# A hybrid attention and mLSTM layer in fp32: the first token tile's norm and its gains' way onto the partitions

## The reference

```
def rms_norm(x, g):
    xf = x.astype(jnp.float32)
    y = xf * lax.rsqrt(jnp.mean(xf * xf, axis=-1, keepdims=True) + EPS)
    return (y * g.astype(jnp.float32)).astype(x.dtype)
...
    xn = rms_norm(h, norm_mix[l])
    proj = xn @ w_in[l]
```

## Time and profile before

| | us |
|---|---|
| median of 3 runs | 950.24 |
| lowest, highest | 948.61, 951.85 |
| profiled execution, its time | 950.14 |
| profiled execution, its span | 948.4 |
| TensorE busy | 936.2 (99% of the span) |
| VectorE busy | 544.2 (57%) |
| ScalarE busy | 415.6 (44%) |
| GpSimd busy | 14.7 (2%) |

### The profile page before, as it was taken

How to read it: one execution, slowest core, us unless ns; L and a number is a source line. 1 busy time by engine, 2 the same in 40 slices (tenths; PEclk the granted TensorE clock), 3 DMA queues, 4 the chain that set the end, 5 groups by cost and what they waited for, 6 DMA issues and landing times.

```text
span 948.4 us, 11911 instructions
## 1 busy us (share of the span) xinstructions
PE 936.2 (99%) x4667; PEld 764.4 (81%) x4667; DVE 544.2 (57%) x942; ACT 415.6 (44%) x694; POOL 14.7 (2%) x39
## 2 busy tenths in 40 slices
PE   8999999999999999999999999999999999999997
PEld 6878777777777878889988778998888888888886
DVE  5532676343546763778333534568847866885543
ACT  5431566344423333344434533366446445634523
POOL 4000000000000000000000000000000000000000
PEclk9999999999999999999999999999999999999999
DMA  8411221122111272342521242120531261062202
GB/s 292 134 46 44 89 90 45 45 89 89 45 45 45 89 258 77 130 135 92 198 89 39 97 175 83 51 89 1 178 134 45 89 222 45 1 207 104 89 1 88
DMA packets 44815, 92.62 MB, mean 98 GB/s; under 512 B 1772, under 2 KB 1864, under 8 KB 44760
## 3 DMA queue, kind: packets, MB, share of 16 engines
q1 hardware_dynamic: 43192, 86.54, 27.1%
q0 software_dynamic: 1568, 5.32, 1.7%
HBM read 89.76 MB, written 2.10 MB: 97 GB/s over the span
## 4 chain that ended last, share of the span: by engine, by line
PE 94%; DVE 3%; ACT 1%; DMA 1%; issue 0%; SPq 0%; ACTq 0%; DVEq 0%
PE bank L1442 70%; PE bank L1473 12%; PE bank L1647 1%; PE bank L1598 1%; PE bank L1541 1%; PE bank L1568 1%; PE bank L1553 1%; PE bank L1486 1%; DVE w_lo L1046 1%; PE bank L1585 1%; PE bank L1625 1%; PE bank L1612 1%; DMA stage<-in_w_in 1%; PE bank L1586 0%; PE bank L1543 0%
## 5 line engine op out<-in xcount | busy, mean ns | idle before, releaser
L1046 DVE TENSOR_TENSOR w_lo<-stage,w_hi 128x1024 fp32r<-128x1024 f32 x174 | 205.0, 1220 | 87.5 <-ACT w_hi L763 87.1
L1442 PE MATMUL bank<-act_hi,w_hi 128*128 128x512 f32 (+1 forms) x640 | 248.3, 388 | 0.1
L1442 PE MATMUL bank<-act_hi,w_lo 128*128 128x512 f32 (+1 forms) x640 | 243.4, 380 | 0.0
L1442 PE MATMUL bank<-act_lo,w_hi 128*128 128x512 f32 (+1 forms) x640 | 243.1, 380 | 0.0
L763 ACT ACTIVATE w_hi<-stage 128x1024 fp32r<-128x1024 f32 x174 | 174.3, 1051 | 96.0 <-PE bank L1442 36.0
L1442 PEld LDWEIGHTS bank<-act_hi,w_lo 128*128 128x128 f32 x640 | 120.7, 189 | 23.3
L1442 PEld LDWEIGHTS bank<-act_hi,w_hi 128*128 128x128 f32 x640 | 121.1, 189 | 22.1 <-DVE w_lo L1046 0.6
L1442 PEld LDWEIGHTS bank<-act_lo,w_hi 128*128 128x128 f32 x640 | 121.0, 189 | 21.4
L1442 PE MATMUL bank<-w_hi,act_hi 128*128 128x512 f32 (+1 forms) x264 | 103.5, 392 | 3.2 <-DVE act_lo L1264 3.2
L1442 PE MATMUL bank<-w_hi,act_lo 128*128 128x512 f32 (+1 forms) x264 | 101.6, 385 | 0.0
L1442 PE MATMUL bank<-w_lo,act_hi 128*128 128x512 f32 (+1 forms) x264 | 101.6, 385 | 0.0
(11 more groups left out here) (276 smaller groups left out, 1261.4 us busy)
## 6 DMA issues: line engine op xcount, KB each, us to landing
stage<-in_w_in SPq DMA_DIRECT2D x20, 1024.0 KB, 5.0
stage<-in_w_mlp_in SPq DMA_DIRECT2D x16, 1024.0 KB, 5.2
stage<-in_w_mlp_out SPq DMA_DIRECT2D x16, 1024.0 KB, 5.5
stage<-in_w_xkv SPq DMA_DIRECT2D x8, 1024.0 KB, 4.9
stage<-in_w_mix_out SPq DMA_DIRECT2D x4, 1024.0 KB, 5.0
stage<-in_w_xq SPq DMA_DIRECT2D x4, 1024.0 KB, 5.1
stage<-in_w_xo SPq DMA_DIRECT2D x4, 1024.0 KB, 4.9
x_tok<-in_x SPq DMA_DIRECT2D x4, 512.0 KB, 9.7
```

What stands on the lines that cost most here:

```text
L1046: dve.tensor_tensor(w_lo[:, r:r + 2, :], stage_pair(pair), w_hi[:, r:r + 2, :].bitcast(F32), ALU.subtract).then_inc(s_low, 1)
L1442: ins = pe.matmul(dst, still[q], moving[q], start=(k == 0 and q == 0), stop=(k == nk - 1 and q == 2))
```

## The change

Tile 0 alone takes another way. VectorE multiplies x by the gains as soon as both are there, without the root (`scale_first`). The root then goes into a 128x128 matrix `eye`, the identity with each row times its root, and TensorE multiplies each 128x128 block of the scaled tile by `eye`, which turns it and applies the root in one fp32 product. The gains of all four tiles are no longer spread by the DMA: ScalarE's queue loads one row of 4 KB into one partition of `row_a`, and TensorE multiplies it by a row of ones into banks 6 and 7, from which VectorE reads them. The 15 first products become 6 ahead of the spread, 4 behind it and 2 behind the turned tile. GpSimd's six small transfers wait until the last x tile has landed.

```
-WARM_UP = 15
+WARM_UP = (6, 4, 2)
...
             load_x(0)
-            sp.dma_start(row_a[:], norm_mix.partition_broadcast(P)).then_inc(s_row_x, 16)
...
+            pool.wait_ge(s_xt[NT - 1], 16)
             small(w16[:, :, 0:8], w_in[:, C_FF:C_FF + 8].rearrange("(k p) n -> p k n", p=P))
...
+            act.dma_start(row_a[0:1, :], norm_mix.rearrange("(o n) -> o n", o=1)).then_inc(s_gains, 16)
             act.wait_ge(s_eps, 1)
...
+            def scale_first(n):
+                dve.wait_ge(s_xt[n], 16)
+                for h in range(2):
+                    c = slice(HALF_W * h, HALF_W * (h + 1))
+                    dve.wait_ge(s_row_x, h + 1)
+                    dve.tensor_tensor(scaled[:, n, c], x_tok[:, n, c], bank[6 + h][:], ALU.mult).then_inc(s_scaled, 1)
+
             def norm_root(n):
                 st = stat[:, n % 2, :]
+                if n == 0:
+                    scale_first(n)
                 dve.wait_ge(s_squares, n + 1)
...
             def norm_scale(n):
                 st = stat[:, n % 2, :]
+                if n == 0:
+                    dve.wait_ge(s_const, N_IDENT)
+                    dve.tensor_scalar(eye[:], ident[:], st[:, 2:3], None, ALU.mult).then_inc(s_eye, 1)
+                    return
+                if n < NT:
+                    for h in range(2):
+                        c = slice(HALF_W * h, HALF_W * (h + 1))
+                        dve.scalar_tensor_tensor(scaled[:, n % 2, c], x_tok[:, n, c], st[:, 2:3], bank[6 + h][:],
+                                                 ALU.mult, ALU.mult).then_inc(s_scaled, 1)
+                    return
...
                 if n == 0:
-                    pe.wait_ge(s_const, N_IDENT)
+                    pe.wait_ge(s_eye, 1)
+                    for b in range(2):
+                        for q in range(4):
+                            k = 4 * b + q
+                            ins = pe.matmul(bank[2 + b][:, P * q:P * q + P], scaled[:, 0, P * k:P * k + P], eye[:],
+                                            start=True, stop=True)
+                        ins.then_inc(s_nturn, 1)
+                    for _ in range(WARM_UP[2]):
+                        pe.matmul(bank[5][:, 0:P], ones[:], ones[:], start=True, stop=True)
+                    return
...
             pe.wait_ge(s_const, 1)
-            for _ in range(WARM_UP):
+            for _ in range(WARM_UP[0]):
                 pe.matmul(bank[7][:, 0:P], ones[:], ones[:], start=True, stop=True)
+            pe.wait_ge(s_gains, 16)
+            for h in range(2):
+                pe.matmul(bank[6 + h][:], ones[0:1, :], row_a[0:1, HALF_W * h:HALF_W * (h + 1)], start=True, stop=True)\
+                  .then_inc(s_row_x, 1)
+            for _ in range(WARM_UP[1]):
+                pe.matmul(bank[5][:, 0:P], ones[:], ones[:], start=True, stop=True)
```

More of the change, by code:

```diff
@@ L423, in trunk @@
         second_sum = sb("second_sum", [P, 1])
+        eye = sb("eye", [P, P])
         first_bias = sb("first_bias", [P, NT])
@@ L505, in trunk @@
         s_residual = sem("s_residual")
+        s_gains, s_eye = sem("s_gains"), sem("s_eye")
         s_row_x, s_row_a, s_row_b = sem("s_row_x"), sem("s_row_a"), sem("s_row_b")
@@ L852, in norm @@
                 c = slice(0 if n < NT + 2 else HALF_W if n < 4 * NT + 1 else HALF_W + EDGE, DM)
-                act.activation(junk[:, n % 2, c], norm_source(n)[:, c], ACT.Square, accum_out=stat[:, n % 2, 0:1])\
+                act.activation(junk[:, 1 if n == 0 else n % 2, c], norm_source(n)[:, c], ACT.Square, accum_out=stat[:, n % 2, 0:1])\
                     .then_inc(s_squares, 1)
```

## The result

Over 22 executions each the median is 951.93 us (950.5 to 955.68) with the change and 949.49 (948.55 to 951.85) before. The ratio is 1.0023, with a 95% interval of 1.0015 to 1.003: slower by 0.23%, within the 0.3% that was called "same". The profiled execution with the change took 954.1 us against 950.14, so it lost 4.0 us where the medians lie 2.4 apart. Both figures need an explanation.

The account below looks back on a forecast made before the run. TensorE holds 94% of the chain of waits, but a ScalarE and VectorE series ends the first 24 products. The second `act_hi` comes 1.64 us later, other terms count nothing: 950.14 + 1.64 = 951.8 us, range 948.7 to 953.6.

Parts of the forecast that it names:

- first part: First 20 us: a chain of ScalarE and VectorE, not TensorE's rate, ends the first two halves' 24 products.
- step 5: ScalarE's second `act_hi` starts at 10.98 instead of 9.34; the first 24 products end 1.64 us later.
- Steps 1 and 2: TensorE's start: six `ones` products until 3.60, then the gains' spread, 3.4 us until 7.00, with 0.21 of drain.
- Step 3: VectorE: multiply stands before the root; second multiply from 7.23, root 0.83, `eye` 0.28, ready at 8.98.
- Step 4: TensorE's turned tile: 16 records at full clock, 1.94 us from 9.02 to 10.96; 3.6 below full clock.
- rival B: TensorE's clock stays low until after the turned tile, 3.6 not 1.94 us: +3.3, 953.4; chance 0.15.
- The case of the forecast: The spread sits in front of VectorE's root, turned tile at full clock: 951.8; chance 0.62.
- Step 6: Removed 512 KB transfer: first weights land at about 6.5, but nothing is gained, since VectorE is busy until 8.98.
- Step 7: Full clock behind the turned tile saves seven products 1.4 us, lost waiting for the fourth `w_lo`: counted as nothing.
- Steps 2 and 8: Spread 3.4 us; delayed small transfers cost nothing; gains from PSUM -0.1 to +0.1 per half, hidden behind TensorE.

Follow-up runs that it names:

- e1: Changed kernel with TensorE's spread and late small transfers kept, but tile 0 scaled and transposed as before: 950.41 us against 950.16 for the kernel before, ratio 1.0.
- e2: Changed kernel without the spread: gains by the 512 KB transfer again, tile 0 still turned by products with `eye`; 951.78 us, ratio 1.0023 to the kernel before.
- e5: Changed kernel with tile 0's root and `eye` ahead of the multiply and no `ones` between spread and turned tile: 952.48 us, ratio 1.0019 to the kernel before.
- e9: Changed kernel with the spread taken over all 128 rows, `row_a` zeroed first: 952.9 us, ratio 1.003 to the kernel before.
- experiment 4: Changed kernel with ScalarE's second `w_hi` ahead of its two `act_hi`: 952.95 us, ratio 1.0029 to the kernel before.
- experiment 6: Kernel before with ScalarE's third `w_hi` ahead of tile 1's squares and seed: 950.37 us, ratio 1.0002.
- experiment 7: e1 with ScalarE's second `w_hi` ahead of `act_hi` and third ahead of tile 1's squares: 949.36 us against 950.39 for the kernel before, ratio 0.9988.
- experiment 11: Experiment 7's kernel with x tile 1 loaded behind the first half of the second lot of weights: 948.78 us against 950.25 for the kernel before, ratio 0.9987.
- experiment 3: Kernel before with its 15 first products taken from one partition in place of 128: 950.56 us, ratio 1.0006.
- experiment 8: The changed kernel once more, unaltered, for a second profile: 954.11 us over 6 executions, ratio 1.0036 to the kernel before.
- experiment 12: Experiment 6's kernel with x tile 1 loaded behind the first half of the second lot of weights: 950.04 us against 950.05 for the kernel before, ratio 1.0003.
- experiment 10: Experiment 7's kernel with the spread over all 128 rows: 949.83 us, ratio 0.9997 to the kernel before.

## Why the prediction was right, and where it was not

**The median, the side and the class.** Forecast 951.8, measured 951.93, in the range and within 0.3%. Against the median of before in the same measurement, 949.49, the loss is 2.4 and not 1.6. That the number fits so well is luck. The sum starts from 950.14, an execution with the slow stretch near 86 us, and adds 1.64; the measured median lies, by its mean clock of 0.998, among executions without that stretch, which lose more at the start. Set beside like executions of the kernel before, the change lost 4.0 us in the profiles, so the terms below were too small by 2.34, and the median hides it.

**What bounds the start** (first part, step 5). Right. From the second `act_hi` to the end of the 24 products it took 8.93 to 8.96 us before, in the change, and in e1, e2, e5 and e9, at either clock of the turned tile, and 0.9 less when one `w_hi` was taken out (experiment 4). The 4.0 us that `act_hi` lost are lost at the end. But TensorE is close behind the series: with a long slow stretch it sets the end itself (experiments 6, 7 and 11).

**Steps 1 and 2, the spread.** Its four records took 3.78 where 3.6 with drain was expected, and began at 3.92 instead of 3.60: 0.5 late together, the size right. One partition makes it no cheaper: 0.22 a record in experiment 3, as with 128. The Trainium skill, "TensorE: Matmul & The Clock Gate", section "Why this matters for your kernels", says the same of 32 rows, and the runs agree.

**Step 3, VectorE.** Right: 1.72 from the second multiply to `eye`, 1.75 expected.

**Step 4, the turned tile: mis-sized.** The prediction took 1.94, at full clock, and kept 3.6 for rival B. The profile has 3.78. With the 0.5 of the spread that is 2.34 more than forecast at the second `act_hi`. Where the clock is up, the term is right (2.05 in e2 and e9). So in both profiles of the change the likeliest case was B, the loss on the side of slower, with B's reason: the one-row products. B was given 0.15; 8 of the 28 executions measured lie at 954 or above. Of the others, 11 fit B's start without the stretch near 86 us, and 9 fit a clock that is up at the spread and low again at the turned tile (experiment 8, an estimate). The case of the forecast, a slow spread and then a turned tile at full clock, stands in no profile of the change.

**Step 6, the 512 KB.** Right that it gains nothing: the first `w_hi` starts 1.95 earlier (5.95, where 6.5 was expected), and behind it ScalarE waits 4.63 for the turned tile.

**Step 7, the clock.** Right for halves 0 and 1: they ran at full clock and gained nothing, since they waited for `w_lo`. The Trainium skill, "TensorE: Matmul & The Clock Gate", Part 4, says that transposes don't count for the clock, and the prediction took this as a reason to think that it would hold. The runs don't need the rule for the falls at the start: in experiments 4 and 7 the clock fell at about 7.4 and 7.8 with no transpose ahead of it, in or behind 0.72 and 1.67 us without work, and before at 10.42, inside a wait of 2.16 behind the transposes. The idle time was not tried apart from them.

**Steps 2 and 8, gains in PSUM and small transfers.** With the spread itself no more than 0.33 at the `fox_v` copy (experiment 1).

**Missed altogether:** the slow stretch near 86 us. It stands in the trace of before, moves a single time by 1.65, and makes a good part of the scatter between executions.

## What to carry to other kernels

Shorten a start at the engine whose series ends it. Here products that spare VectorE one wait were put in front of ScalarE's series, while 2.1 to 4.6 us of ScalarE's idle time stood unused beside it; two kernels that use that time are 0.12 and 0.13% faster than the kernel before by their medians, though their profiled executions don't show it at the start. A step that another engine can compute while the first operand is still on its way (the root) belongs ahead of the wait, not behind. And where executions lie in groups, read the effect in the profile at a fixed point behind the change, since a median of six or eight can be off by a whole group.

## What was not expected of the hardware

- Products from one partition kept TensorE busy without bringing its clock up: 30 of their records from 1.05 to 7.8, and the lower level until 15.8; with 128 rows of the same operands it was up by 7.0. The spread over all rows, with zeros in 127 of them, was followed by full clock (experiment 9). Products from one partition can run at full clock, though, where it is already up: the spread took 2.02 and 2.18 in experiments 4 and 7, behind the same 12 records of `ones` as in the change.
- The clock rises at another time in another execution of the same instructions: the 15 first products took 6.44 in the kernel before, 5.16 and 5.08 in experiments 6 and 12.
- A 4 KB transfer on ScalarE's queue was there by 3.9 when issued at 0.80, and not before 7.4 when issued at 2.03, or 6.9 in experiment 10, in the midst of the transfers of x and weights.
- The clock fell once more at 86 us in most profiles, behind many small products of 12 columns, with no idle time of TensorE in the rows; in experiments 3, 9, 10 and 11 it did not. What decides between the two was not tried.
